# Five open quads of experts instead of four, and one y buffer, in a hybrid trunk layer with 32 experts

## The reference

```python
# t = rmsnorm(h) (256, 2048); combine (256, 32): weight of each expert per token, 0 for 30 of them
for e in range(N_EXPERTS):
    hdn = jax.nn.silu(t @ w1[e]) * (t @ w3[e])                 # w1, w3: (2048, 512)
    out = out + combine[:, e:e + 1] * (hdn @ w2[e])            # w2: (512, 2048)
h = h + out
pe = rmsnorm(p[i] @ w_ple[i], g_ple[i])
gate = jax.nn.sigmoid(rmsnorm(h, g_pg[i]) @ w_pg[i] + b_pg[i]) # w_pg: (2048, 2048)
h = h + gate * pe
```

## Time and profile before

| what | value |
|---|---|
| median of three runs | 1380.48 us |
| profiled execution, its own time | 1380.46 us |
| its span in the trace | 1378.6 us |
| PE busy | 1089.6 us (79%) |
| VectorE (DVE), ScalarE (ACT) busy | 285.3 us, 156.6 us |
| DMA over the whole span | 476.14 MB, mean 345 GB/s |
| chain that ended last | DMA 52%, PE 44% |
| first open expert to last, then pieces | the quads end near 1174 us, the last store is issued near 1376 us |

### The profile page before, as it was taken

How to read it: one execution, slowest core, us unless ns; L and a number is a source line. 1 busy time by engine, 2 the same in 40 slices (tenths; PEclk the granted TensorE clock), 3 DMA queues, 4 the chain that set the end, 5 groups by cost and what they waited for, 6 DMA issues and landing times.

```text
span 1378.6 us, 13825 instructions
## 1 busy us (share of the span) xinstructions
PE 1089.6 (79%) x6016; PEld 506.1 (37%) x6016; DVE 285.3 (21%) x439; ACT 156.6 (11%) x314; POOL 53.4 (4%) x66
## 2 busy tenths in 40 slices
PE   8999999999876688576766567666666566899998
PEld 4458887445532233222222123222222221333333
DVE  1104725512321222112221111000000000111116
ACT  1111315002200012000000000000000000010002
POOL 0103100200000002000000000000000000000000
PEclk9999999999897899878888878888888888899999
DMA  9943333364599999999999999999999999999991
GB/s 352 307 153 123 123 123 127 127 242 183 192 427 427 426 430 426 428 427 428 427 427 428 426 427 427 415 427 428 412 426 425 418 428 412 392 396 388 396 356 61
DMA packets 91053, 476.14 MB, mean 345 GB/s; under 512 B 10272, under 2 KB 10416, under 8 KB 67952
## 3 DMA queue, kind: packets, MB, share of 16 engines
q1 hardware_dynamic: 84896, 471.88, 84.5%
q0 software_dynamic: 560, 2.88, 0.6%
q10 hardware_dynamic: 5536, 0.47, 0.3%
HBM read 473.12 MB, written 2.10 MB: 345 GB/s over the span
## 4 chain that ended last, share of the span: by engine, by line
DMA 52%; PE 44%; SPq 2%; DVE 1%; issue 1%; ACT 0%; DVEq 0%
DMA ring<-in_w 52%; PE ps L1421 8%; PE ps L1384 6%; PE ps L1674 5%; PE ps L1545 4%; PE ps L1558 4%; PE ps L1754 4%; PE ps L1851 4%; PE ps L1646 2%; PE ps L1809 1%; SPq L452 1%; PE ps L1639 1%; SPq L386 1%; PE ps L1822 1%; PE ps L1578 1%
## 5 line engine op out<-in xcount | busy, mean ns | idle before, releaser
L1754 PE MATMUL ps<-ring,area 128*32 128x512 f32 x1024 | 165.3, 791 | 123.3 <-DMA ring<-in_w 122.3
L1674 PE MATMUL ps<-ring,area 128*32 128x512 f32 x976 | 148.5, 727 | 123.8 <-DMA ring<-in_w 123.8
L1184 DVE TENSOR_TENSOR h<-ps,h 128x2048 f32<-128x2048 f32 x32 | 73.3, 2292 | 298.8 <-PE ps L1646 298.8
L1754 PEld LDWEIGHTS ps<-ring,area 128*32 128x32 f32 x1024 | 43.5, 137 | 231.3 <-issue 231.3
L1421 PE MATMUL ps<-hT,ring 128*128 128x256 f32 x512 | 112.9, 380 | 0.0
L1674 PEld LDWEIGHTS ps<-ring,area 128*32 128x32 f32 x976 | 31.6, 122 | 221.6 <-issue 221.2
L1421 PEld LDWEIGHTS ps<-hT,ring 128*128 128x128 f32 x512 | 96.5, 190 | 14.0 <-issue 1.2
L1384 PE MATMUL ps<-ring,hT 128*128 128x512 f32 x192 | 85.6, 606 | 1.1 <-DVE hT L907 1.1
L1851 PE MATMUL ps<-ring,area 128*128 128x512 f32 x176 | 79.8, 595 | 3.5 <-ACT area L871 3.1
L1229 DVE TENSOR_TENSOR hT<-area,ps 128x128 f32<-128x128 f32 x16 | 4.6, 288 | 315.9 <-ACT area L860 315.9
L1639 PE MATMUL ps<-area,hs 128*128 128x128 f32 x512 | 66.6, 285 | 0.5 <-DVE area L1165 0.5
(11 more groups left out here) (278 smaller groups left out, 795.8 us busy)
## 6 DMA issues: line engine op xcount, KB each, us to landing
ring<-in_w SPq DMA_DIRECT2D x157, 2048.0 KB, 21.2
ring<-in_w SPq DMA_DIRECT2D x59, 1024.0 KB, 14.6
ring<-in_w_in SPq DMA_DIRECT2D x28, 1024.0 KB, 12.4
ring<-in_w_out SPq DMA_DIRECT2D x16, 1024.0 KB, 7.4
ring<-in_w_pg SPq DMA_DIRECT2D x11, 1024.0 KB, 14.2
area<-in_w SPq DMA_DIRECT2D x2, 2048.0 KB, 14.1
hs<-in_w SPq DMA_DIRECT2D x4, 1024.0 KB, 15.2
hs<-in_w_pg SPq DMA_DIRECT2D x3, 1024.0 KB, 17.5
```

The lines of the kernel that those rows point to most:

```text
L1184: dve.tensor_tensor(h[:, t, :], ps[:, bank:bank + 4, :].rearrange("p b n -> p (b n)"), h[:, t, :], ALU.add).then_inc(acc_done, 1)
L1674: ins = mm(ps[SLOTS * g:SLOTS * g + SLOTS, 0, :], XG[:, b, k, SLOTS * e:SLOTS * e + SLOTS], s[:, D_EXP * kk:D_EXP * kk + D_EXP], start=(k ...
L1754: ins = mm(ps[SLOTS * g:SLOTS * g + SLOTS, 0, :], XG[:, b, k, SLOTS * e:SLOTS * e + SLOTS], s[:, D_EXP * kk:D_EXP * kk + D_EXP], start=(k ...
```

## The change

`OPEN_QUADS` goes from 4 to 5, so experts 12 to 15 are open too, and three quads are full. The pieces have 5 x 4 chunks of w2 each. Three things follow by hand: the gate units are spread over five quads by a formula (2, 1, 2, 1, 1, and one behind the last scatter); the half of XG with which the open quads begin is the other one, so that the last quad again reads the upper half (`FIRST_XG`); and HDNs now takes 0 to 2560 of `hT_flat`, four G matrices 2560 to 3584, the fifth a free part of `area`, which leaves room for one y buffer. With one buffer, `copy_y` of step m waits for the scatter of step m - 1 instead of m - 2.

```diff
-OPEN_QUADS = 4
+OPEN_QUADS = 5
+PIECE_CHUNKS = 4 * OPEN_QUADS + 4
+FIRST_XG = FULL_QUADS % 2
...
-    return OPEN_CHUNKS + 20 * (i - 1) + 4 * q + k + 1
+    return OPEN_CHUNKS + PIECE_CHUNKS * (i - 1) + 4 * q + k + 1
...
-    return OPEN_CHUNKS + 20 * i + 16 + kk + 1
+    return OPEN_CHUNKS + PIECE_CHUNKS * i + 4 * OPEN_QUADS + kk + 1
+
+def gate_units(q):
+    return range(-(-7 * q // OPEN_QUADS), -(-7 * (q + 1) // OPEN_QUADS))
...
-        Gs = hT_flat[:, 2048:2048 + OPEN_QUADS * T].rearrange("p (q t m) -> p q t m", q=OPEN_QUADS, t=NT)
-        Ys = hT_flat[:, 3072:4096].rearrange("p (b n) -> p b n", b=2)
+        G_HOMES = [hT_flat[:, 2560 + T * q:2560 + T * q + T] for q in range(4)] + [part(10240, T)]
+        Gs = [g_.rearrange("p (t m) -> p t m", t=NT) for g_ in G_HOMES]
+        Y = hT_flat[:, 3584:4096]
...
-                if m >= 2:
-                    act.wait_ge(piece_ps, m - 1)
-                act.activation(Ys[:, m % 2, :], ps[:, 4 + m % 2, :], ACT.Copy).then_inc(y_copied, 1)
+                if m >= 1:
+                    act.wait_ge(piece_ps, m)
+                act.activation(Y, ps[:, 4 + m % 2, :], ACT.Copy).then_inc(y_copied, 1)
...
-                    spread(1 - q % 2, e, j, 1, open_gather, open_xg)
+                    spread(1 - (q + FIRST_XG) % 2, e, j, 1, open_gather, open_xg)
...
-                b = q % 2
+                b = (q + FIRST_XG) % 2
...
-                    ins = mm(ps[:, 6 + t, :], Gs[:, q, t, :], Ys[:, m % 2, :], start=(q == 0), stop=(q == OPEN_QUADS - 1))
+                    ins = mm(ps[:, 6 + t, :], Gs[q][:, t, :], Y, start=(q == 0), stop=(q == OPEN_QUADS - 1))
...
                 for q in range(OPEN_QUADS):
-                    gate_unit(i - 1, 2 * q)
-                    if q < OPEN_QUADS - 1:
-                        gate_unit(i - 1, 2 * q + 1)
+                    for u in gate_units(q):
+                        gate_unit(i - 1, u)
                     w2_piece(i, q)
```

More of the change, by code:

```diff
@@ L856, in _ @@
                     act.wait_ge(open_g_ps, j // QUAD + 1)
-                    act.activation(Gs[:, j // QUAD, :, :], ps[:, 3, 0:T].rearrange("p (t q) -> p t q", t=NT), ACT.Copy
+                    act.activation(Gs[j // QUAD], ps[:, 3, 0:T].rearrange("p (t q) -> p t q", t=NT), ACT.Copy
                                    ).then_inc(open_g, 1)
@@ L1185, in accumulate, with first_quad @@
                                   ).then_inc(acc_done, 1)
-            def first_quad(g0):
+            def first_quad(g0, b=0):
                 for q in range(4):
-                    spread(0, q, g0 + q, 1 + q % 2)
+                    spread(b, q, g0 + q, 1 + q % 2)
             def quad_of(n0, g0, slots, quad, b, begins=False):
@@ L1287, in _ @@
                     select(slice(0, QUAD), slot_x)
-                    first_quad(gathers)
+                    first_quad(gathers, FIRST_XG)
                     with dve.Fori(0, QUADS // 2) as i:
                         for b in range(2):
-                            quad_of(r * NE + FULL, gathers, slot_x, i * 2 + b, b)
+                            quad_of(r * NE + FULL, gathers, slot_x, i * 2 + b, (b + FIRST_XG) % 2)
                 dve.nop()
@@ L1720, in expert_of, with first_gathers @@
                     ins.then_inc(chunks_used, 1)
-            def first_gathers(g0, s0, count):
+            def first_gathers(g0, s0, count, b=0):
                 pe_.wait_ge(sel_ready, s0 + 1)
@@ L1726, in first_gathers @@
                         pe_.wait_ge(xg_ready, g0 + (q - 1))
-                    gather(0, q, 1 + q % 2)
+                    gather(b, q, 1 + q % 2)
             def open_loaded_pair(g):
@@ L1875, in _ @@
                     pe_.wait_ge(xg_ready, gathers)
-                    first_gathers(gathers, selects, 4)
+                    first_gathers(gathers, selects, 4, FIRST_XG)
                     with pe_.Fori(0, QUADS // 2) as i:
@@ L1879, in _ @@
                             for e in range(QUAD):
-                                expert_of(r * NE + FULL, gathers, selects, i * 2 + b, e, b)
+                                expert_of(r * NE + FULL, gathers, selects, i * 2 + b, e, (b + FIRST_XG) % 2)
                 pe_.nop()
```

## The result

The changed kernel takes 1387.27 us, the median of seven runs (1384.42 to 1388.74), against 1380.43 us of seven runs before (1379.95 to 1383.58). The ratio is 1.004 with a 95% interval of 1.0029 to 1.0051: slower, by 4 to 7 us. The profiled execution takes 1387.35 us, its span is 1385.6 us, against 1380.46 and 1378.6 before.

The account below looks back on a forecast made before the run. DMA was taken to bound the kernel up to the last w2 chunk, with a tail that no load decides. The terms were 1380.46 + 4.0 (short runs) + 0.7 (copy's wait) = 1385.2 us, range 1381.0 to 1389.5.

Parts of the forecast that it names:

- What bounds the kernel: Up to the last w2 chunk DMA sets the pace: 427 GB/s in 16 KB runs, 388 in 2 KB w2 pieces.
- The price of 16 chunks: w2 of experts 12 to 15 moves to 2 KB rows: 4.0 us more on the path, bounds 0 and 4.2.
- The check by the period: turn_piece spacing of 53.2 us against DMA's 16 x 2.70 + 4 x 2.46 = 53.0 us per piece.
- The fifth quad on PE: Extra w2 and scatter per piece, 5.4 us of PE, hidden under 7.1 us of slack; uncovered 16.2 us.
- The copy's wait: One y buffer, between the last two scatters of piece 3: 0.7 us in the tail, bounds 0 and 2.1.
- The sum: Whole kernel: 1380.46 + 4.0 + 0.7 = 1385.2 us, 0.34% more.
- the stretch from 1384.3 to 1386.2: Span of total times in us assigned to the forecast itself, with chance 0.59.
- the clock as a rival: TensorE's clock drops after PE's waits in pieces or tail: 3.4 us, giving 1388.6, at worst 1392; chance 0.17.
- The Trainium skill's rule: DMA transfers of 512 B and more reach line rate, so the short runs cost 0: 1381.2 us.
- The prediction's estimate of 4%: Short-run cost from three extra cycles per packet, 67/64 against 515/512: 1.6 us, sum near 1382.8.
- The rival on the faster side: 388 GB/s in the pieces is PE's doing, so the last w2 lands 11.5 us earlier: 1369.7 us; chance 0.06.
- The hidden price: Row length of the moved w2 loads costs mostly nothing, only the copy shows: 1381.2 us; chance 0.14.

Follow-up runs that it names:

- run 1: Kernel before, with only the w2 loads of full experts 12 to 15 in runs of 2 KB instead of 16 KB (wrong weights): 1385.52 us, ratio 1.0034.
- run 5: Kernel before, four open quads, with all 64 w2 piece chunks read in runs of 8 KB (wrong weights): 1372.81 us, ratio 0.9943.
- run 6: Changed kernel, five open quads, with all 80 w2 piece chunks read in runs of 8 KB (wrong weights): 1367.73 us, ratio to before 0.9917.
- run 10: Kernel before with the w2 loads of experts 3 to 15 in runs of 2 KB (wrong weights): 1395.71 us, ratio 1.0109.
- run 4: The changed kernel measured and profiled again, nothing altered: 1385.66 us, ratio to the kernel before 1.0034.
- run 3: Changed kernel, five open quads, with a second y buffer, so the copy waits for the scatter before the last: 1386.38 us, ratio to before 1.0036.
- Run 2: Kernel before, four open quads, with one y buffer, so only the copy's wait of the change: 1381.6 us, ratio 1.0005.
- run 7: Changed kernel with three open quads (five full) and two y buffers: 1384.68 us, ratio to the kernel before 1.0034.
- run 8: Changed kernel, five open quads, with two y buffers and all eight gate units ahead of w2: 1382.44 us, ratio to before 1.0018.
- run 9: Kernel before, four open quads and two y buffers, with all eight gate units ahead of w2: 1387.13 us, ratio 1.0054.

## Why the prediction was right, and what it missed

- What bounds the kernel: right. DMA set the pace up to the last w2 chunk in both kernels, and 388 GB/s is what 2 KB runs allow. Runs 1, 5, 6 and 10 show it from both sides.
- The price of 16 chunks, forecast 4.0 us: of the 6.0 us at the last landing 2.0 were there at the first w2 product, so 4.0 are left. In run 4 it is 6.06 - 1.89 = 4.2, in run 3 7.42 - 3.42 = 4.0 (landings 1340.49 and 1341.85). Run 2, with four quads, has 952.5 us from the front to that landing against 952.4 before, so a shifted front moves the landing with it. The check by the period had one term off: w_pg was taken at 427 GB/s, but run 5 shows 421 for 8 KB runs. With 2.49 us for a w_pg chunk a piece is 16 x 2.70 + 4 x 2.49 = 53.2 us, the measured period.
- The fifth quad on PE, forecast as hidden: right. PE waited more, not less. That PE's own 51.3 us came so near to the 51.5 of run 5 is partly luck. PE is busy for 50.5 us of that period, and the other 1.02 us are the wait for ACT behind the turn, which the prediction took off as idle though PE can't do without it.
- The copy's wait, forecast 0.7 us in the tail and 0 elsewhere: the place was right, the size 1.0. The step that failed took the gap from the row, 0.69 us, as the whole cost. The scatters begin 1344.20 - 1341.47 = 2.73 us apart, and 1.82 in run 3: 0.91 us. Of these 0.75 are the gap; a scatter takes 1.98 us, so back to back the second begins 0.16 us ahead of the first one's end, and this overlap is lost.
- The sum, 4.7 us: the lowest times of the first series differ by 1384.42 - 1379.95 = 4.5, the medians by 6.8. In the profiled execution the missing 2 us are the front. The median of 1387.27 lies above the stretch from 1384.3 to 1386.2 that had been given 0.59; it is in the stated range because that was left wide for other rivals, which is luck. Run 4's 1385.66, the same kernel, lies in that stretch. The prediction had looked for the clock as a rival in the pieces and the tail alone. It named that rival's mechanism correctly (the clock did fall in the pieces, 0.89 and 0.94 in two windows, and was repaid there; in the tail it stood at 1.00), but at a place where nothing hides it, the projection ahead of the experts, it was not looked for.
- The Trainium skill's rule (DMA: Bandwidth & Descriptors, Specifications) that 512 B reach line rate would have put the sum at 1381.2. The runs don't agree: 2 KB runs moved 386 to 388 GB/s, 8 KB runs 421 and 16 KB runs 427. The prediction's estimate of 4%, 1.6 us, is too small as well; 427 against 388 is 10%, and the profiles show 4.0 us.
- The rival on the faster side, that 388 GB/s is PE's doing, is refuted by run 1 and by run 5, where PE takes 20 chunks in 51.5 us, 407 GB/s. Its argument against it, the share of 1.05, was weaker than it looked: in runs 5 and 7 PE was the bound and the share stayed at 1.01 and 1.04.
- The hidden price is refuted by the last landing, 4.0 us later than the front explains, and by run 1.

## What to carry to other kernels

Regrouping work so that another engine's load balances better is a change of DMA too: before counting the slack that it opens, count the bytes that move to shorter runs and multiply by the difference of the two rates in the trace. Where two engines are within a few per cent of each other, a small wait is hidden on the side with slack and paid at every turn on the other, as the same edit showed in runs 8 and 9. And when profiles of two kernels are compared, first see how much of the difference is already there in code that the change doesn't touch.

## What the runs showed that I had not expected

The DMA share was highest with the shortest runs: 16 KB 1.01 and 427 GB/s, 8 KB 1.01 and 421, 2 KB 1.05 and 387. In the pieces a share well below 1 came only where the loads were at their end (0.78 in run 7). Where PE set the pace with loads still to come, the share stayed above 1. It told whether loads were under way, not which side was the bound; the waits and the distance of the turns told that.

The clock in the stage ahead of the experts differs between executions of the same code, with PE busy in either case, and moves what is behind it: the first w2 product began between 380.79 and 385.46, 4.7 us apart. With a median of few runs this is as large as the effect of many an edit. Why the clock falls there in some executions stays open.
